# Forming the low part of the second half of each weight unit on GpSimd, with a semaphore for each half

## The reference, cut to what matters

```python
mods = jnp.einsum('bd,lde->lbe', jax.nn.silu(c), ada_w) + ada_b[:, None, :]
h = rms_norm(x, norm_w[i, 0]) * (1 + sc_m) + sh_m
y = ab_mixer(h, ...) or cd_mixer(h, ...)      # proj = h @ w_in ... concatenate(...) @ w_out
x = x + g_m * rms_norm(y, norm_w[i, 1])
h = rms_norm(x, norm_w[i, 2]) * (1 + sc_f) + sh_f
y = conv_ffn(h, ...)                          # (gelu(gate) * val) @ w_down, gate and val from h @ w_up
x = x + g_f * rms_norm(y, norm_w[i, 3])
```

## Time and profile before

| what | value |
|---|---|
| median of 3 runs | 1261.04 us (1260.23 to 1261.66) |
| span of the profiled execution, first to last instruction | 1258.0 us |
| median less the span: what lies around it | 3.0 us |
| mean granted TensorE clock | 0.958 |
| TensorE matmuls busy | 1153.8 us, 92% |
| VectorE busy | 883.5 us, 70% |
| ScalarE busy | 627.7 us, 50% |
| GpSimd busy | 21.0 us, 2% |
| DMA: mean rate | 155 GB/s |

### The profile page before, as it was taken

How to read it: one execution, slowest core, us unless ns; L and a number is a source line. 1 busy time by engine, 2 the same in 40 slices (tenths; PEclk the granted TensorE clock), 3 DMA queues, 4 the chain that set the end, 5 groups by cost and what they waited for, 6 DMA issues and landing times.

```text
span 1258.0 us, 28100 instructions
## 1 busy us (share of the span) xinstructions
PE 1153.8 (92%) x10161; PEld 1116.5 (89%) x10161; DVE 883.5 (70%) x1909; ACT 627.7 (50%) x1317; POOL 21.0 (2%) x12
## 2 busy tenths in 40 slices
PE   5899999979799999979999988599987898999996
PEld 5899988979799999979999976599977897999996
DVE  3588547669778889967887755844443886888854
ACT  1376554354466664445666453155423445666542
POOL 0000000000000000000000001300100000000000
PEclk9799899999899999979999999799999898999998
DMA  9356533518545557814764520012200682555561
GB/s 363 136 179 238 180 136 108 199 68 318 218 141 182 181 182 276 291 52 138 248 216 138 180 68 2 1 54 84 69 1 2 219 305 66 180 183 183 183 193 60
DMA packets 54830, 195.58 MB, mean 155 GB/s; under 512 B 6067, under 2 KB 8115, under 8 KB 54492
## 3 DMA queue, kind: packets, MB, share of 16 engines
q1 hardware_dynamic: 54748, 194.45, 44.9%
HBM read 193.36 MB, written 1.07 MB: 155 GB/s over the span
## 4 chain that ended last, share of the span: by engine, by line
PE 69%; DVE 6%; ACT 2%; issue 1%; DVEq 0%; ACTq 0%
PE proj L507 44%; PE acc L507 24%; DVE off_bd L1677 1%; DVE state L1751 1%; DVE yr L1469 0%; PE acc L688 0%; DVE sys_t L1685 0%; DVE yr L1492 0%; DVE o_tok L1778 0%; DVE k_tok L1667 0%; DVE conv L1698 0%; DVE w_lo L1345 0%; ACT w_hi L1003 0%; DVE ada_sum L1359 0%; DVE dec L1660 0%
## 5 line engine op out<-in xcount | busy, mean ns | idle before, releaser
L1003 ACT ACTIVATE w_hi<-raw 128x512 fp32r<-128x512 f32 x528 | 328.5, 625 | 198.6 <-PE acc L507 146.7
L1345 DVE TENSOR_TENSOR w_lo<-raw,w_hi 128x512 fp32r<-128x512 f32 x528 | 358.8, 684 | 79.2 <-ACT w_hi L1003 78.1
L507 PE MATMUL proj<-h_hi,w_hi 128*128 128x256 f32 x1352 | 389.2, 288 | 4.4 <-DVE h_lo L1465 3.9
L507 PE MATMUL proj<-h_lo,w_hi 128*128 128x256 f32 x1352 | 385.6, 285 | 0.0
L507 PE MATMUL proj<-h_hi,w_lo 128*128 128x256 f32 x1352 | 385.5, 285 | 0.0
L507 PEld LDWEIGHTS proj<-h_hi,w_hi 128*128 128x128 f32 x1352 | 262.5, 194 | 7.7 <-issue 4.2
L507 PEld LDWEIGHTS proj<-h_lo,w_hi 128*128 128x128 f32 x1352 | 262.9, 194 | 0.0
L507 PEld LDWEIGHTS proj<-h_hi,w_lo 128*128 128x128 f32 x1352 | 262.6, 194 | 0.0
L507 PE MATMUL acc<-a_hi,w_hi 128*128 128x256 f32 (+1 forms) x608 | 172.5, 284 | 3.7 <-DVE a_lo L1632 2.0
L507 PE MATMUL acc<-a_lo,w_hi 128*128 128x256 f32 (+1 forms) x608 | 170.9, 281 | 0.0
L507 PE MATMUL acc<-a_hi,w_lo 128*128 128x256 f32 (+1 forms) x608 | 170.4, 280 | 0.0
(11 more groups left out here) (259 smaller groups left out, 1629.9 us busy)
## 6 DMA issues: line engine op xcount, KB each, us to landing
raw<-in_w_stream SPq DMA_DIRECT2D x264, 512.0 KB, 3.4
ada_long<-in_ada_stream SPq DMA_DIRECT2D x52, 512.0 KB, 7.0
ada_first<-in_ada_stream SPq DMA_DIRECT2D x20, 512.0 KB, 4.2
ada_ssd<-in_ada_stream SPq DMA_DIRECT2D x12, 512.0 KB, 4.4
ada_out<-in_ada_stream SPq DMA_DIRECT2D x12, 512.0 KB, 4.7
hankel<-bias_scratch SPq DMA_DIRECT2D x2, 1024.0 KB, 5.8
x<-in_x_tiles SPq DMA_DIRECT2D x1, 1024.0 KB, 10.4
out_tiles<-x SPq DMA_DIRECT2D x1, 1024.0 KB, 3.9
```

The lines of the kernel that those rows point to most:

```text
L507: return pe.matmul(out, a, b, start=start, stop=stop, skip_group_check=True)
L1003: act.activation(hi, src, ACT.Copy).then_inc(w_rounded, 1)
L1345: dve.tensor_tensor(lo, src, hi.bitcast(F32), ALU.subtract).then_inc(w_split, 1)
```

## The change

The low part of half a = 1 of every unit is formed by GpSimd, and that of half a = 0 stays with VectorE. `w_split` becomes a pair of semaphores, one per half, which each count units. SyncE waits for both before it loads over a unit; TensorE waits for the one of its half. GpSimd's other work keeps its order and its waits, and the new subtractions are set around it: those up to z1 ahead of the wait for the attention (`s_ready`), z1 0 and 1 behind the two `conv1` products, z1 2 up to out1 1 behind the clearing of `step_y_bd`, and the rest at the end. `split_half` on VectorE returns at once for a = 1.

```diff
-        w_rounded, w_split, w_used = sem("w_rounded"), sem("w_split"), sem("w_used")
+        w_rounded, w_used = sem("w_rounded"), sem("w_used")
+        w_split = [sem("w_split_first"), sem("w_split_second")]
...
                 if n >= 4:
-                    sp.wait_ge(w_split, 8 * i + 2 * n - 6)
+                    for a in range(2):
+                        sp.wait_ge(w_split[a], 4 * i + n - 3)
...
                     for a in range(2):
-                        pe.wait_ge(w_split, 8 * i + 2 * n + a + 1)
+                        pe.wait_ge(w_split[a], 4 * i + n + 1)
...
             def split_half(n, a, i=0):
-                if n >= UNITS:
+                if n >= UNITS or a:
                     return
                 hi, lo, src = w_half(n, a)
                 dve.wait_ge(w_rounded, 8 * i + 2 * n + a + 1)
-                dve.tensor_tensor(lo, src, hi.bitcast(F32), ALU.subtract).then_inc(w_split, 1)
+                dve.tensor_tensor(lo, src, hi.bitcast(F32), ALU.subtract).then_inc(w_split[0], 1)
...
         @block.gpsimd
         def _(pool):
+            def split_second(n, i=0):
+
+                hi, lo, src = w_half(n, 1)
+                pool.wait_ge(w_rounded, 8 * i + 2 * n + 2)
+                pool.tensor_tensor(lo, src, hi.bitcast(F32), ALU.subtract).then_inc(w_split[1], 1)
+
+            def split_all(n0, n1):
+
+                groups = (n1 - n0) // 4
+                with pool.Fori(0, groups) as i:
+                    for j in range(4):
+                        split_second(n0 + j, i)
+                for n in range(n0 + 4 * groups, n1):
+                    split_second(n)
+
+            n_z1 = PARTS["z1"][0]
             pool.memset(c_silu[:, :, :], 0.0).then_inc(c_zeroed, 1)
+            split_all(0, n_z1)
             pool.wait_ge(s_ready, 8)
...
                 pool.tensor_tensor(t, t, egc[:, b * GH:b * GH + GH], ALU.mult).then_inc(g_scaled, 1)
+            for n in range(n_z1, n_z1 + 2):
+                split_second(n)
             pool.wait_ge(g_scaled, 4)
             pool.memset(step_y_bd[:, :, :], 0.0).then_inc(zeroed, 1)
+            for n in range(n_z1 + 2, n_z1 + ZT + 2):
+                split_second(n)
             pool.wait_ge(i_z_mm, 3 * (LEVELS - 2))
             pool.wait_ge(i_off, 3 * LEVELS)
             pool.memset(v_new[:, :, :, :, :], 0.0).then_inc(zeroed, 1)
             pool.memset(resid[:, :, :, :, :], 0.0).then_inc(zeroed, 1)
+            split_all(n_z1 + ZT + 2, UNITS)
```

More of the change, by code:

```diff
@@ L576, in project_values @@
                     for a in range(2):
-                        pe.wait_ge(w_split, 2 * (n0 + k) + a + 1)
+                        pe.wait_ge(w_split[a], n0 + k + 1)
                         hi, lo, _ = w_half(n0 + k, a)
```

## The result

The kernel after takes **1297.87 us** (three of its four executions lie between 1297.59 and 1298.09; the fourth took 3823.53 us and is left out of the comparison), against 1260.63 us for the kernel before in the same session. The ratio is 1.0294, 95% interval 1.0278 to 1.031. The change costs 37 us; 12.6 were forecast. The span of the profiled execution is 1295.5 us at a mean granted clock of 0.959, so TensorE's clock is on average what it was (0.958).

What follows compares the result with a forecast made beforehand. TensorE was taken to bound the kernel (69% of the chain, VectorE 6%). Stages with ada terms 7.2 + start 0.9 + out0's third unit 1.9 + k1 0.5 + DeltaNet 2.1 = 12.6 us on 1261.0 gave 1273.6 us, range 1264 to 1289.

Steps and rivals of the forecast that it cites:

- Edits at nothing: Conv and up stages, SyncE's second wait, GpSimd's queue: cost nothing; conv and up taps read PSUM, VectorE has 0.5 us spare.
- waits of TensorE in conv: Sign named for a wrong forecast: TensorE waiting in conv and up, which were costed at nothing.
- The ring's slack: Stages with ada terms: the ring of four halves hides 2.5 us of each stage's loss, leaving 7.2 us in all.
- The four-unit stages: q0, q1 and down1, four units with terms each: lose 1.3 us each, under the 2.5 hidden, so nothing.
- The hold: VectorE instructions with two SBUF inputs: each GpSimd subtraction holds VectorE up to 1.07 us and saves it 0.60.
- rival 2: Only tensor_tensor is held, not the ada terms' scalar_tensor_tensor: +2.4 us, about 1263.5 us; chance 0.16.
- rival 3: Nothing is held and the change helps at the start, ahead of v0 and in k1: -3.0 us, 1258; chance 0.07.
- GpSimd's length: One 128x512 subtraction on GpSimd takes 1.21 us, against 0.68 on VectorE; 1.2 to 1.7 with turns.
- Rival 1: GpSimd's instruction is longer; from 1.5 us on the ada stages pay in full: 1280 to 1292 us; chance 0.19.
- The single places: Places on VectorE's path: start +0.9, ahead of out0's third unit +1.9, k1 +0.5, DeltaNet +2.1 us.
- out0's entry: Ahead of out0's third unit: GpSimd's subtractions delay the low part TensorE waits for, +1.9 us.
- nothing here would be held: Skill's 2-port rule, read alone: no 2-port mode for tensor_tensor, so no holds and 1258 us; the trace disagreed.

Runs made afterwards that it cites:

- e1: Kernel after, but in the conv stages VectorE forms the first half's low part ahead of ScalarE's first tap: 1279.56 us, ratio 1.015.
- e4: Kernel after with the halves exchanged, GpSimd forming the first half's low part and VectorE the second's: 1287.72 us, ratio 1.0192.
- e2: Kernel after, but VectorE forms both low parts in the stages with ada terms (60 of 264 units): 1282.08 us, ratio 1.0159.
- e5: Kernel after, but GpSimd does each of its subtractions twice and reports only the second: 1399.46 us (one execution).
- e6: Kernel after, but GpSimd copies raw to w_lo (one input) in place of subtracting, so results differ: 1256.77 us (one execution).
- e10: Kernel after with the eight ada terms for v0's unit issued inside k0, VectorE's instruction order staying the same: 1295.78 us, ratio 1.0278.
- e3: Kernel after with the edits of e1 and e2 together, and GpSimd's first two z1 halves ahead of its DeltaNet work: 1265.37 us, ratio 1.0021.
- e7: Kernel before, no GpSimd subtractions, with eight ada terms issued inside k0 instead of between k0 and v0: 1256.58 us, ratio 0.9952.
- e9: e8 with the eight ada terms issued inside k0, VectorE's instruction order staying the same: 1258.05 us, ratio 0.9975.
- e8: e3 with the first two units and out0's units 2 and 3 also on VectorE, 200 subtractions left to GpSimd: 1260.28 us, ratio 0.9976.

## Why the prediction was wrong, and where it was right

**The step that failed is "Edits at nothing": the conv stages.** It said that the taps have a PSUM input and that VectorE has some 0.5 us a unit to spare. Both are so (480 ns; e1). But the low part between the taps has two inputs in SBUF, and I had counted time per unit where the question was when the instruction stands against its user. VectorE's first low part waits in order behind a tap, which waits for ScalarE's tap, which waits for TensorE's end of the unit; by then 1.4 us of the 2.88 to its use have gone, and the subtraction takes 0.68 of the rest. A hold of 1.1 us on this one instruction passes the 0.8 us that is left, whatever the spare time of the unit. The prediction had named waits of TensorE in conv as a sign of being wrong, and they came. The forecast priced this at nothing, and conv is 17.5 of the 24.9 us that were missed (some 0.9 of it, an estimate, is TensorE at its lower level for 4.4 us at conv1's start in place of 2.7). e1 shows it: the same work in another order brings them back. The up stages, put at nothing in the same sentence, did cost nothing, by where GpSimd's half falls in the unit; e4 shows the other case.

**The ring's slack failed as a size, and a term was missing beside it.** I took 2.5 us off each stage with terms. In down0 nothing came off: TensorE waits 1.45 us for a low part already at its third unit, and the stretch loses 6.0 us, ten pairs at 6.70 us by VectorE (forecast 6.77) against 6.09 by TensorE. In out0 the slack was about what I took, with two slow units of TensorE to help VectorE: the next five pass unharmed and the waits cost 2.2 us against 1.5. Its 4.15 us come near 12 x 0.335 = 4.0, but by luck, for 2.7 of them are TensorE's clock behind the wait ahead of the third unit, which the forecast doesn't have. The four-unit stages, which were to vanish in the slack, lost too: q0's stretch 1.7, up1 with down1 2.7. For the latter e2, which takes GpSimd's share out of the units with terms, gives only 0.3 back in the whole stretch (211.9 us) and 1.5 from its norm on (202.7 to 201.2); the rest wasn't looked into.

**The hold was right.** 1.03 us measured per subtraction for 1.07, on scalar_tensor_tensor as on tensor_tensor: rival 2, by which the terms escape, falls, and so does rival 3. The Trainium skill, SBUF — State Buffer, under "SBUF: two separate sides", calls the shared pair an exclusive lock that is held for the whole instruction. By that rule, the trace agrees with the turns of the earlier trace rows and of e5. The balance of what is held and what is saved hangs on GpSimd's length, as e6 shows.

**GpSimd's length was 7% low.** 1.30 us alone (1.258 the shortest) for 1.21, and 1.506 in the mean with the turns, inside the 1.2 to 1.7 that was named; busy 418.7 us for 350 to 450. Rival 1 has its sign from this and from TensorE's waits, but its mechanism, the length of the instruction, isn't what decided: at 1.30 us conv costs nothing in e1.

**The single places.** Two are confirmed: k1 +0.6 (forecast 0.5; +0.6 in e1, e4 and e10 too, 0.0 in e2 and e3, where VectorE has both low parts there) and out0's entry, whose wait grew by 1.75 us (1.9). Two have the size that was forecast and aren't shown. The start took +1.1 (0.9), but it takes 47.8 us in e1 and 44.8 in e10, whose program is the same there, and 44.6 in e7, whose program is that of the kernel before. DeltaNet took +1.2 (2.1), but 150.5 us in e1, with the same program and the same holds, against before's 151.0. VectorE does meet the two z1 subtractions as forecast; what their holds cost isn't known. L1695 in after, first with GpSimd idle, then with the z1 subtractions beside it:

```profile
815.68 0.69 DVE L1695 TENSOR_TENSOR inv_t<-sys_t,cst 128x512 f32<-128x512 f32 x1
...
826.11 1.65 DVE L1695 TENSOR_TENSOR inv_t<-sys_t,cst 128x512 f32<-128x512 f32 x1
```

**A remark on one sum.** The prediction says that with a length of 1.11 us in place of 1.21 the sum would come out within 1 us. That holds only with some 0.1 us of fixed cost on top; with 1.11 alone its own terms would give about 8 us, not 12.6.

**Not in the forecast at all: the clock.** The attention, dt1 and the lengths of layer 1 moved by -3.6, -1.9 and +2.9 us without a change in their work, and out0 lost 2.7 by it. For the attention, the place of the eight terms for v0's unit is shown to matter (e7); that the clock is what links the two is read from the windows and not tried by itself.

## What to carry to other kernels

Before work goes to GpSimd, list VectorE's instructions with two SBUF inputs in the time that GpSimd will be busy, and ask of each one how long before its use it ends, not how much time its engine has to spare per unit; the one whose use comes first must be clear of GpSimd, by the order of issue if need be. GpSimd's own length is the price: a subtraction of 1.30 us that saves VectorE 0.60 and holds it 1.03 loses wherever VectorE has no gap. And a TensorE-bound kernel gains little from a VectorE with less to do, while one wait of 1.2 us moved away was worth 3.4 us in its own stretch (e7; 5.6 by the medians, of which some 2 may be chance, as e9 and e10 show).

## What the runs showed of the hardware that was not expected

- **A one-input instruction of VectorE in float32 is held as well.** In after, a `tensor_scalar` of 128x128 takes 0.28 us, and 1.29 when it meets a subtraction:

```profile
170.45 0.28 DVE L1527 TENSOR_SCALAR scores<-scores,small 128x128 f32<-128x128 f32 x1
...
170.83 1.29 POOL L1898 TENSOR_TENSOR w_lo<-raw,w_hi 128x512 fp32r<-128x512 f32 x1 [4.20 <-ACT w_hi L1005]
170.91 1.29 DVE L1527 TENSOR_SCALAR scores<-scores,small 128x128 f32<-128x128 f32 x1
```

  The Trainium skill, Advanced Engine Details and Errata, VectorE Performance Modes, lists a 2-port mode for tensor_scalar and says that such instructions and GpSimd's block each other; by that rule, the trace agrees. One ada term in eight is a `tensor_scalar`, so that the prediction's "nothing here would be held" passed over it; in after those of `ada_first` take 492 ns in the mean, 347 before.
- **GpSimd's copy of 128x512 takes 0.62 us and its subtraction 1.30**, each where VectorE lets it run; with the second input and the subtraction it takes twice as long.
- **The same wait is followed by either level of the clock.** Behind a wait of TensorE for `conv` of 2.71 us, layer 1's lengths take 10.08 us in before and 13.00 in e3; the granted clock is 1.00 in the first and 0.50 in the second (columns as above):

```profile
717.00:721.00 4.00, 2.04 (x18) 2.04 (x19) 3.83 (x11) 1.85 (x3) 0.00 (x0) 1.00 0.05 20
```

```profile
720.00:724.00 4.00, 4.00 (x19) 4.00 (x20) 2.60 (x5) 0.00 (x0) 0.00 (x0) 0.50 0.00 0
```

  In after the wait is 3.25 us, the clock 0.50 in 746:750, and the lengths take 13.02. In twelve kernels this stretch has three lengths: 10.1 us in before, e1, e2, e4 and e7, 13.0 in after, e3, e8, e9 and e10, and 11.4 in e5 and e6. What decides between them isn't settled; no run changed the wait ahead of it alone.
